# Token rows gathered ahead in four quarters, results scattered to token rows, turns by VectorE, one-run down weights

## The reference, cut to what matters

```python
def hierarchical_moe(x, w_group, b_group, w_router, b_router, w1, w3, w2):
    ...  # top-1 group of 8, then the top-2 experts of its 8; 64 experts in all
    def expert_block(args):
        xb, e = args
        return (jax.nn.silu(xb @ w1[e]) * (xb @ w3[e])) @ w2[e]
    ...
    y_sorted = yb.reshape(-1, d)[dest] * sorted_w[:, None].astype(x.dtype)
    y = jnp.zeros((t, d), x.dtype).at[sorted_tok].add(y_sorted)
```

## Time and profile before

| | |
|---|---|
| time, median of 3 runs | 2192.16 us (2192.0 to 2193.31) |
| the profiled execution's own time | 2188.43 us |
| its span, first to last instruction | 2186.3 us |
| TensorE busy | 1819.5 us, 83% |
| VectorE, ScalarE, GpSimd busy | 477.7, 252.1, 245.0 us |
| read from and written to HBM | 479.84 and 34.35 MB |

### The profile page before, as it was taken

The page is one execution under the profiler, slowest core; times in us unless marked ns, Lnnn a source line. Parts: engine busy times, 40 slices in busy tenths (PEclk is TensorE's granted clock), DMA queues, the critical chain, the costliest instruction groups (busy, mean ns, idle before and its releaser), DMA issues.

```text
span 2186.3 us, 39333 instructions
## 1 busy us (share of the span) xinstructions
PE 1819.5 (83%) x13926; PEld 994.2 (45%) x13927; DVE 477.7 (22%) x1147; ACT 252.1 (12%) x543; POOL 245.0 (11%) x375
## 2 busy tenths in 40 slices
PE   7999999999999999999757567777777777676774
PEld 3676456644444444445534234444444444443442
DVE  5618214511110111146510000011011010001015
ACT  4012314200000000011100000000000000000002
POOL 1951000000000000001111011011111111111112
PEclk9999999999999999999779788899899888888898
DMA  6320321201111110073669999898999999999996
GB/s 194 145 61 22 128 77 34 68 2 43 43 43 43 43 43 38 0 288 122 250 265 419 419 413 401 346 406 339 407 401 403 405 401 410 408 399 407 410 365 237
DMA packets 152792, 510.97 MB, mean 234 GB/s; under 512 B 34400, under 2 KB 84064, under 8 KB 135840
## 3 DMA queue, kind: packets, MB, share of 16 engines
q1 hardware_dynamic: 122096, 461.36, 54.5%
q0 software_dynamic: 8816, 27.02, 3.5%
q10 hardware_dynamic: 21840, 22.06, 2.9%
HBM read 479.84 MB, written 34.35 MB: 235 GB/s over the span
## 4 chain that ended last, share of the span: by engine, by line
PE 59%; DMA 17%; ACTq 7%; SPq 5%; issue 4%; DVE 3%; ACT 2%; POOLq 0%; POOL 0%; DVEq 0%
PE act_bank L772 27%; PE dve_bank L772 15%; DMA unit_results<-lane_row 6%; PE act_bank L1114 5%; DMA unit_results<-spatialT 4%; ACTq L1328 4%; DMA gain_b<-xf_rows,gather_idx 4%; PE dve_bank L779 4%; PE act_bank L1100 3%; SPq L575 3%; SPq L520 2%; PE dve_bank L1114 2%; DMA tokens<-expert_token_table 1%; SPq L524 1%; ACTq L410 1%
## 5 line engine op out<-in xcount | busy, mean ns | idle before, releaser
L772 PE MATMUL act_bank<-norm_store,unit 128*128 128x512 f32 x1024 | 449.8, 592 | 0.2 <-DMA unit<-in_w_in 0.2
L772 PEld LDWEIGHTS act_bank<-norm_store,unit 128*128 128x128 f32 x1024 | 194.0, 190 | 239.4 <-issue 238.4
L1100 PE MATMUL act_bank<-unit,gain_a 128*32 128x256 f32 x3200 | 186.9, 385 | 24.5 <-issue 23.9
L1114 PE MATMUL act_bank<-unit,gain_a 128*32 128x256 f32 x2432 | 202.9, 490 | 0.0
L1846 DVE TENSOR_TENSOR gain_a<-gain_a,act_bank 128x128 f32<-128x128 f32 x100 | 28.8, 288 | 773.0 <-ACT gain_a L1321 765.0
L779 PE MATMUL dve_bank<-ident,gain_a 128*128 128x128 f32 x100 | 35.2, 352 | 169.2 <-DVE gain_a L1846 167.2
L1100 PEld LDWEIGHTS act_bank<-unit,gain_a 128*32 128x32 f32 x3200 | 109.3, 112 | 105.3 <-issue 49.8
L779 PE MATMUL dve_bank<-ident,gain_b 32*128 32x32 f32 x808 | 78.2, 242 | 77.4 <-DMA gain_b<-xf_rows,gather_idx 77.3
L1681 DVE TENSOR_TENSOR rows_store<-dve_bank,rows_store 128x512 f32<-128x512 f32 x48 | 33.3, 693 | 431.0 <-PE dve_bank L772 431.0
L1114 PEld LDWEIGHTS act_bank<-unit,gain_a 128*32 128x32 f32 x2432 | 95.1, 135 | 63.8 <-issue 42.5
L719 POOL DMA_INDIRECT gain_b<-xf_rows,gather_idx x101 | 94.3, 934 | 248.3 <-PE dve_bank L779 240.0
(11 more groups left out here) (268 smaller groups left out, 1507.8 us busy)
## 6 DMA issues: line engine op xcount, KB each, us to landing
unit<-in_w SPq DMA_DIRECT2D x112, 2048.0 KB
norm_store<-in_w SPq DMA_DIRECT2D x32, 2048.0 KB
mid_store<-in_w SPq DMA_DIRECT2D x32, 2048.0 KB
rows_store<-in_w SPq DMA_DIRECT2D x16, 2048.0 KB
unit<-in_w_gate SPq DMA_DIRECT2D x24, 512.0 KB, 5.2
unit<-in_w_in SPq DMA_DIRECT2D x4, 2048.0 KB, 8.7
unit_results<-unit POOLq DMA_DIRECT2D x4, 2048.0 KB, 13.4
unit_results<-lane_row ACTq DMA_DIRECT2D x200, 32.0 KB
```

The costliest lines, as they stand in the source:

```text
L772: ins = nc.tensor.matmul(out_, stationary, moving, start=first and n == 0, stop=n == len(pairs) - 1)
L1100: ins = nc.tensor.matmul(act_bank[0][h * CAP:(h + 1) * CAP, 0:2 * FQ].rearrange("t (w n) -> t w n", w=2), xT[:, k], w13[s][:, :, k, h * FQ ...
L1114: ins = nc.tensor.matmul(y_bank[s][z * CAP:(z + 1) * CAP, 0:DQ], hidT[:, j], w2s[s][:, j, z * DQ:(z + 1) * DQ], start=j == 0, stop=j == QU ...
```

## The change

The rows of a token are treated as four quarters of 256 columns, and a unit's 32 tokens as 128 rows of 1 KB, one for each partition. Nothing of the arithmetic changes.

- **Gathers.** GpSimd fetches 128 rows of 1 KB in each indirect DMA. For each expert it fetches unit 0 in `open_expert` (two experts ahead: it first adds the quarter's number to the token list with a TENSOR_SCALAR) and unit 1 in `open_next`; while unit c is worked on it fetches unit c+2 of the same expert. The gathers are issued whether the expert has such a unit or not: rows that don't exist have an index beyond the bounds and aren't moved. That makes 66 + 66 + 100 = 232 gathers in place of 101.
- **Results.** GpSimd scatters each unit's result in one indirect DMA of 128 rows of 1 KB to the row of its token and choice in `choice_results`; ScalarE issues no stores. At the end SyncE loads 8 tiles of 1 MB in plain DMAs. The indices for it are a second column of the table, and `y_row` and its computation go.
- **Turns.** VectorE turns 32 x 32 blocks (`transpose`) of the gathered rows into `xT`, and of `hid` into `hidT`. TensorE's turns in the loop and the copies from PSUM go. The norm writes its rows unpermuted.
- **Down weights** come in one run of 16 KB for each partition.
- **Token lists** are loaded by ScalarE three experts ahead, in 4 DMAs each (one for each quarter of the partitions, 8 KB).
- The 4 DMAs that cleared the result rows early in the kernel go.

```diff
+                    e = t * SLOTS + s
+                    first = eng.value_load(spans[0:1, 0, bass.ds(e, 1)], min_val=0, max_val=SLOT_UNITS)
+                    end = eng.value_load(spans[0:1, 0, bass.ds(e + SLOTS, 1)], min_val=0, max_val=SLOT_UNITS)
+                    shift = eng.value_load(spans[0:1, 1, bass.ds(e, 1)], min_val=0, max_val=UNITS)
                     if enter:
-                        enter(s, t)
+                        enter(s, t, first + shift)
                     with eng.Fori(first, end) as c:
-                        u = nc.s_assert_within(c + shift - less if less else c + shift, 0, UNITS - 1, skip_runtime_bounds_check_because=(
-                            "the units of all experts are at most UNITS"))
-                        body(c, s, u, t, first)
+                        body(c, s, c + shift, t, first)
+                    if leave:
+                        leave(s, t, end, end + shift)
+
+        def turns_at(u, s, t):
+
+            return u + t * SLOTS + (s + 1)
...
             def expert_down(w_down, s):
-                sp.dma_start(w2s[s], w_down.rearrange("e (k p) n -> p (e k) n", p=P)).then_inc(down_loaded[s], 16)
+                sp.dma_start(w2s[s].rearrange("p k n -> p (k n)"), w_down.rearrange("e (p k) n -> p (e k n)", p=P)
+                             ).then_inc(down_loaded[s], 16)
...
                 expert_down(down, s)
@@ -582,19 +594,23 @@
                 for s in range(SLOTS):
                     refill(t * SLOTS + s, s)
 
...
-            sp.wait_ge(per_slot["gu_ready"][0], last)
+            last = [sp.value_load(spans[0:1, 0, E + s:E + s + 1], min_val=0, max_val=SLOT_UNITS) for s in range(SLOTS)]
+            sp.wait_ge(per_slot["gu_ready"][0], last[0])
...
-
+            for s in range(SLOTS):
+                sp.wait_ge(per_slot["y_stored"][s], last[s] * 16 + 16)
             for i in range(NT):
-                b = i % PICKS
+                sp.dma_start(y_both[i], y_tiles[i]).then_inc(row_loaded[i], 16)
+
+            for i in range(NT):
...
-                        token_id[:, i:i + 1], None).then_inc(table_filled, 16)
+                        token_rows[:, i, c], None).then_inc(table_filled, 16)
...
-            def gather(idx, u):
-                pool.wait_ge(tok_gathered, u * 16 + 16)
+            def gather(rows, idx, landed):
+                pool.indirect_dma_start(rows, None, xf_quarters, bass.IndirectOffsetOnAxis(ap=idx, axis=0),
+                                        bounds_check=T * QUARTERS - 1, oob_is_err=False).then_inc(landed, 16)
+
+            def open_expert(s, t):
+
+                f = s % 2
+                pool.wait_ge(tokens_loaded[s], t * (16 * QUARTERS) + 16 * QUARTERS)
                 pool.nop(nofuse=True)
-                nc.gpsimd.tensor_copy(gather_idx[:, :], idx).then_inc(idx_copied, 1)
-                pool.wait_ge(idx_copied, u + 1)
-                pool.wait_ge(tok_turned, u + 1)
-
+                nc.gpsimd.tensor_scalar(tokens[:, s, 0:COLS], token_lists[:, s, 0:COLS], quarter_no[:, 0:1], None,
+                                        ALU.add).then_inc(list_made[f], 1)
+                pool.wait_ge(list_made[f], t * 2 + (s // 2 + 1))
                 pool.nop(nofuse=True)
-                pool.indirect_dma_start(xg, None, xf_dram,
-                                        bass.IndirectOffsetOnAxis(ap=gather_idx[:, 0:1], axis=0),
-                                        bounds_check=T - 1, oob_is_err=False).then_inc(tok_gathered, 16)
-
-            def unit_work(c, s, u, t, first):
+                gather(open_rows[f], tokens[:, s, 0, 0:1], open_landed[f])
+
+            def open_next(s):
+                gather(next_rows[s % 2], tokens[:, s, 1, 0:1], next_landed[s])
+
+            def scatter(c, s, first):
                 column = nc.s_assert_within(c - first, 0, COLS - 1, skip_runtime_bounds_check_because=(
                     "an expert has at most T tokens"))
-                gather(tokens[:, s, bass.ds(column, 1)], u)
...
                 pool.nop(nofuse=True)
-
-            each_unit(pool, unit_work, expert_tokens)
-            units = (pool.value_load(spans[0:1, 1, E - 1:E], min_val=0, max_val=SLOT_UNITS)
-                     + pool.value_load(spans[0:1, 2, E - 1:E], min_val=0, max_val=UNITS))
-            gather(no_token[:, :], units)
-
...
-            def pick(i):
...
-                for c in range(2):
-                    pool.indirect_dma_start(y_pick[b][c], None, y_dram,
-                                            bass.IndirectOffsetOnAxis(ap=y_row[:, c, i:i + 1], axis=0)
-                                            ).then_inc(picked[b], 16)
...
+                nc.gpsimd.tensor_copy(y_idx[:, s:s + 1], tokens[:, s, bass.ds(column, 1), 1]).then_inc(y_indexed[s], 1)
+                pool.wait_ge(y_indexed[s], c + 2)
+                pool.nop(nofuse=True)
+                pool.indirect_dma_start(y_dram, bass.IndirectOffsetOnAxis(ap=y_idx[:, s:s + 1], axis=0), y_rows[s],
+                                        None, bounds_check=2 * T * QUARTERS - 1, oob_is_err=False
+                                        ).then_inc(per_slot["y_stored"][s], 16)
+
+            def unit_work(c, s, u, t, first):
+                f = s % 2
+                column = nc.s_assert_within(c - first + 2, 0, COLS + 1, skip_runtime_bounds_check_because=(
+                    "an expert has at most T tokens"))
+
+                pool.wait_ge(xT_ready, turns_at(u, s, t) + 1)
+                pool.nop(nofuse=True)
+                nc.gpsimd.tensor_copy(next_idx[:, f:f + 1], tokens[:, s, bass.ds(column, 1), 0]
+                                      ).then_inc(next_indexed[s], 1)
+                pool.wait_ge(next_indexed[s], c + 1)
+                pool.nop(nofuse=True)
+                gather(next_rows[f], next_idx[:, f:f + 1], next_landed[s])
+                scatter(c, s, first)
...
+
+            def enter(s, t, u):
+                pool.wait_ge(xT_ready, turns_at(u, s, t))
+                pool.nop(nofuse=True)
+                open_expert(*ahead(s, t))
+
+            def leave(s, t, end, units):
+                pool.wait_ge(next_landed[s], (end + t) * 16 + 16)
+                pool.nop(nofuse=True)
+                open_next(ahead(s, t)[0])
+
+            for s in range(AHEAD):
+                open_expert(s, 0)
+                open_next(s)
+            each_unit(pool, unit_work, enter, leave)
...
-                pe.wait_ge(per_slot["hid_ready"][s], c + 1)
-                turn(dve_bank[1], [hid]).then_inc(per_slot["hid_turned"][s], 1)
-                turn_tokens(u + 1)
                 pe.wait_ge(per_slot["hidT_ready"][s], c + 1)
...
-                act.sem_inc(per_slot["y_stored"][s], 16 * QUARTERS)
...
-                act.wait_ge(per_slot["y_stored"][s], c * (16 * QUARTERS) + 16 * QUARTERS)
+                act.wait_ge(per_slot["y_stored"][s], c * 16 + 16)
                 nc.scalar.activation(y_rows[s], y_bank[s][:, 0:DQ], ACT.Copy).then_inc(per_slot["y_drained"][s], 1)
-                act.wait_ge(per_slot["y_drained"][s], c + 2)
-                for z in range(QUARTERS):
-                    act.dma_start(y_dram[bass.ds(u * CAP, CAP), z * DQ:(z + 1) * DQ],
-                                  y_rows[s][z * CAP:(z + 1) * CAP]).then_inc(per_slot["y_stored"][s], 16)
-
...
+
+            def list_ahead(s, t, u):
+                at, slot = t * SLOTS + s + LISTS, (s + LISTS) % SLOTS
+                used = act.value_load(spans[0:1, 0, bass.ds(at, 1)], min_val=0, max_val=SLOT_UNITS)
+                chosen_expert = act.value_load(spans[0:1, 2, bass.ds(at, 1)], min_val=0, max_val=E - 1)
+                act.wait_ge(y_indexed[slot], used + 1)
+                load_list(slot, table_of[bass.ds(chosen_expert, 1)].rearrange("e p n -> (e p) n"))
+
+            each_unit(act, unit_work, list_ahead)
...
-            def unit_work(c, s, u, t, first):
+            def turn_tokens(rows):
+                v.transpose(xT, rows.rearrange("p (m k) -> p k m", k=KD)).then_inc(xT_ready, 1)
+
+            def gated(c, s):
                 dve.wait_ge(per_slot["silu_ready"][s], c + 1)
                 v.tensor_tensor(hid, silu_g, act_bank[0][:, FQ:2 * FQ], ALU.mult).then_inc(per_slot["hid_ready"][s], 1)
-                dve.wait_ge(per_slot["hid_turned"][s], c + 1)
-                v.tensor_copy(hidT, dve_bank[1][:, 0:P].rearrange("p (j t) -> p j t", j=QUARTERS)
-                              ).then_inc(per_slot["hidT_ready"][s], 1)
-                take_tokens(u + 1)
-
-            take_tokens(0)
-            each_unit(dve, unit_work)
+                dve.wait_ge(per_slot["hid_ready"][s], c + 1)
+                v.transpose(hidT, hid.rearrange("p (m j) -> p j m", j=QUARTERS)).then_inc(per_slot["hidT_ready"][s], 1)
+
+            def unit_work(c, s, u, t, first):
+                gated(c, s)
+                dve.wait_ge(next_landed[s], (c + t) * 16 + 16)
+                turn_tokens(next_rows[s % 2])
+
+            def leave(s, t, end, units):
```

(26 more changed lines are left out.)

232 lines of the change are left out of this document (103 added, 129 removed).

## The result

The changed kernel takes 2252.52 us (median of 4 runs, 2249.96 to 2258.71) against 2192.08 (4 runs): a ratio of 1.0282, 95% interval 1.0259 to 1.0306, so 60 us slower.

A forecast was written before the change was run, and what follows sets the result against it. The prediction took DMA of weights to bound the kernel, and GpSimd's chain after the change: 2188.4 - 3.5 + 149 - 9 = 2325 us profiled, forecast 2328 for the runs; range 2170 to 2530, 2250 to 2410 for this case alone.

The forecast's parts named there:

- GpSimd becomes the bound through the landing in `leave`: Expert stage: GpSimd's in-order chain, waiting in `leave` some 60 times 4 to 7 us, lengthens the stage by 149 us.
- One-unit expert, 13.9 us when the engines are full: GpSimd's chain per one-unit expert: landing 7.1, `open_next` 1.8, loop ends and value loads 1.8, `open_expert` 2.1, copy and wait 1.1.
- landings in between: Expert stage: T mixes quiet chain 886 us and full chain 1232 by mean DMA share 973/T, giving 1173 us.
- 9.5 us for a further unit: GpSimd's chain inside an expert, engines full: result buffer's loop 9.4, gather's loop 8.6, so 9.5 us; quiet 7.0.
- Down weights -15: Expert stage's DMA work: 16 KB runs take 4.8 instead of 5.1 us per expert, -15 us; some 10 of time.
- Rival B: GpSimd's gathers: 1 KB rows stay apart, 144 packets, landing 10.8 us; stage +370, 2550 us; chance 0.18.
- Rival C: Wait in `leave`: gathers without rows land sooner, 5.5 us; stage +77, 2256 us; chance 0.16.
- Rival A: Expert stage: DMA stays the bound if empty landings take 4.2 us or less; 2160 us; chance 0.15.
- Ends: Outside the expert stage: -3.5 us ahead of it (-1 to -6), -9 us behind it (-5 to -13).

The follow-up runs named there:

- taking the wait away in two ways: Changed kernel with four buffers for the second unit's rows, 2155.82 us; or with two buffers, wait and `open_next` moved into the next expert, 2144.59 us.
- the one with the later wait: Changed kernel, wait for the expert's last gather and `open_next` moved behind the next expert's `open_expert` gather: 2144.59 us, ratio 0.977; again 2143.93 us.

## Why the prediction was wrong in size

- **GpSimd becomes the bound through the landing in `leave`: right**, shown by taking the wait away in two ways (-97 and -108 us) with all gathers kept.
- **One-unit expert, 13.9 us when the engines are full: nearly.** Measured 13.3 in the cycle above: the landing 7.1 and a release 0.8, `open_next` 1.05, value loads 1.02 (I took 1.8), TENSOR_SCALAR 0.45 (0.3), 0.82 + 1.07, copy 0.20 + 0.82.
- **The failed step: "landings in between", that is the mixing by T = 886 + (1232 - 886) x 973/T, and with it the price of a further unit.** It gave every expert 13.2 and every further unit 9.5 x 0.83 + 7.0 x 0.17 = 9.1 us, 327 us for 36. Measured are 1096 - 63 x 13.20 = 264 us, 7.3 each: 63 of the 70 us by which the stage was forecast too long. Some 50 of the 63 are the 19 further units of experts with three units or more, 6.4 us each, whose gathers met idle engines; some 12 are the 17 second units of two-unit experts, 8.35 us each, whose landings met full ones in 15 cases. For one-unit experts the mix was right by luck: their landings did not shorten, their other pieces were 0.6 us less. The engines' idle time is not spread over all landings, as the formula has it, but lies inside the longer experts. The other 7 us lie at the stage's first and last expert and were not looked into; the 2 us by which the start came earlier, and a median 0.2 us below the profiled execution in place of 3.7 above it, make up most of the rest of the 75 us between forecast and measurement.
- **9.5 us for a further unit** with full engines rested on the result buffer's loop. It exists (ScalarE waited 10.47 us for a scatter's landing at 1613.38), but the second units, with full engines, took 8.35: near the 8.6 that the prediction had for the gather's own loop and let the larger number replace.
- **Down weights -15: wrong**, -6 to +4. It rested on two windows of 3 us. By the formula for T it weighed 3.6 us in the forecast, not the 10 that the prediction says.
- **Rival B fell**: 48 packets for each DMA. The Trainium skill, "DMA: Bandwidth & Descriptors", section "SWDGE vs HWDGE vs iDMA", with packets of preferably at most 4096 bytes, is borne out for rows of 1 KB.
- **Rival C** gave 2256 us for landings without rows in 5.5 us. They took 7: its number was met by luck. Its row, the last gather of the earlier trace rows, was quick with the weights gone, not because it had no rows: in the changed kernel all 60 such landings behind weights took 5.9 us or more.
- **Rival A** fell as written, but what it said of the stage once DMA bounds it (2160) is near what the kernels without the wait do (2144 to 2156).
- **Ends**: -5.6 for -3.5 and -8.8 for -9. The tail's plain loads put the first sum at 2216.52, 9.1 us behind the last down matmuls, and all is over 34.5 us later.

The version to keep is the one with the later wait, 2144 us, 2.2% below the kernel before. Its stage lies between these rows:

```profile
1106.86 3.44 PE L1137 MATMUL act_bank<-norm_store,gain_a 128*32 128x256 f32 x36 [15.33 <-DVE gain_a L1872]
...
2093.47 3.64 PE L1148 MATMUL dve_bank<-rows_store,gain_a 128*32 128x256 f32 x32 [3.32 <-issue]
```

Of its gain, 43.2 us of span, 34 are in the stage (1106.86 to 2097.11), 3 ahead of it and 6 behind. That the stage's part comes from fewer result bytes and a chain well below the weights' time is argued, not tested apart.

## What to carry to other kernels

A prefetch that may be empty costs as much in an in-order engine's chain as a full one, once something waits for its landing: find where that wait stands and put work under it, or the wait behind the next step; here one step was worth 108 us. When landings get shorter with less traffic, ask which landing meets which traffic, and don't mix by the mean share: here 60 of 63 landings in `leave` met full engines while the share of the stage was 0.8 to 0.96, and the idle time lay in the few long experts. And a rate from a window of 3 us is no gain over a stage.

## What the runs showed of the hardware

- Four rows of 1 KB gathered or scattered by GpSimd's indirect DMA are one packet (48 packets for 128 rows, also where the rows don't exist). ScalarE's stores of 1 KB rows were one packet each.
- An indirect DMA of 128 rows costs GpSimd 1.05 us against 0.93 for 32 rows, and lands in 7.1 us behind weights, as 32 rows of 4 KB did; with quiet engines within 3.5 us. In between lie 3.5 to 6.4 us at shares of 0.51 to 0.76 between issue and landing.
- 16 KB against 4 KB runs: 418 against 411 GB/s while busy, and no gain clear of the noise in four pairs of kernels (-6 to +4 us).
- VectorE's turn of 128x256 in 32 x 32 blocks, read with a stride, takes 0.62 us against 0.43 for the copy from PSUM; that of 128x128 0.40. Groups of the changed kernel, 1117 to 2200 us:

```profile
L1866 DVE STREAM_TRANSPOSE gain_a<-gain_b 128x256 f32<-128x256 f32 x160 | 99.8, 624 | 151.7 <-DMA gain_b<-xf_rows,next_idx 144.5 <-DVE gain_a L1866 2.1 <-DMA gain_b<-xf_rows,gain_a 0.8
L1872 DVE STREAM_TRANSPOSE gain_a<-gain_a 128x128 f32<-128x128 f32 x98 | 39.5, 403 | 3.4
...
L735 POOL DMA_INDIRECT gain_b<-xf_rows,next_idx x98 | 103.2, 1053 | 83.7 <-POOL next_idx L771 77.4 <-issue 3.2 <-ACT spatialT L1355 3.0
```
